# One matmul of 512 columns with a tile of high weights, or two of 256

## The reference, cut to what matters

```python
proj = u @ w_in[l]                       # 2048 x 9216, then attention and a convolution
... @ w_attn_o[l]; ... @ w_conv_o[l]     # 1024 x 2048 each
h = h + rms_norm(merged @ w_out[l], ...) # 2048 x 2048
gate, up = jnp.split(u @ w_gate_up[l], 2, axis=-1)   # 2048 x 11264
f = (jax.nn.silu(gate) * up) @ w_down[l]             # 5632 x 2048
h = x @ w_in                             # second block, even layer: 2048 x 6144
mixed @ w_out                            # 2048 x 2048
r, k, v, g = xr @ w_r, xk @ w_k, xv @ w_v, xg @ w_g  # odd layer: 2048 x 2048 each
(o + bonus) * silu(g) @ w_o                          # 2048 x 2048
```

## Time and profile before

| | |
|---|---|
| median of 3 runs | 2597.3 us (2593.73 to 2601.03) |
| profiled execution, first to last instruction (its span) | 2597.7 us |
| time of the profiled execution around its span | not recorded apart from the span; the runs and the span agree within 0.2% |
| TensorE matmul busy | 2502.5 us, 96% |
| TensorE weight load busy | 2160.8 us, 83% |
| VectorE busy | 1568.4 us, 60% |
| ScalarE busy | 1175.1 us, 45% |
| DMA | 427.69 MB, mean 165 GB/s |
| granted TensorE clock, mean | 0.988 of full speed |

### The profile page before, as it was taken

One profiled execution on the slowest core, in us unless ns is written; L12 is line 12 of the kernel. 1 busy time (PEld: TensorE's weight loads), 2 busy tenths in 40 slices (PEclk: granted clock), 3 DMA queues, 4 the chain that ended last, 5 costly groups with the idle time before them and its releaser, 6 DMA issues.

```text
span 2597.7 us, 38168 instructions
## 1 busy us (share of the span) xinstructions
PE 2502.5 (96%) x15470; PEld 2160.8 (83%) x15470; DVE 1568.4 (60%) x2116; ACT 1175.1 (45%) x1547; POOL 72.4 (3%) x94
## 2 busy tenths in 40 slices
PE   8999999999899999999999899989899999999896
PEld 7888888888788888888888688878787888888685
DVE  6888887774666655564444657655622674356555
ACT  5444554644444444444444355563546201255544
POOL 0000000000000000000000000000000201011000
PEclk9999999999999999999999999999999999999998
DMA  6564555555366566656555455545633457422362
GB/s 231 185 191 155 159 174 186 164 186 177 95 189 189 181 190 190 189 181 193 184 183 187 130 179 176 174 129 179 195 122 106 142 167 211 128 93 79 116 213 89
DMA packets 419455, 427.69 MB, mean 165 GB/s; under 512 B 25344, under 2 KB 414464, under 8 KB 418320
## 3 DMA queue, kind: packets, MB, share of 16 engines
q1 hardware_dynamic: 414880, 403.07, 49.0%
q0 software_dynamic: 4400, 22.19, 2.6%
HBM read 415.19 MB, written 9.96 MB: 164 GB/s over the span
## 4 chain that ended last, share of the span: by engine, by line
PE 84%; DVE 10%; ACT 4%; issue 1%; DMA 1%; SPq 0%; ACTq 0%; DVEq 0%
PE GP L1791 76%; PE SB L1791 7%; DVE wL L1011 3%; ACT wH L495 2%; DVE y L1011 1%; DVE acc L1017 1%; DVE x L1011 1%; DVE j L1011 1%; DVE f L1017 1%; DVE ga L1011 0%; PE SB L1795 0%; DMA raw<-w_o_dram 0%; DMA raw<-w_in_dram 0%; DVE xk L1017 0%; ACT sc L583 0%
## 5 line engine op out<-in xcount | busy, mean ns | idle before, releaser
L1011 DVE TENSOR_TENSOR wL<-raw,wH 128x1024 fp32r<-128x1024 f32 x664 | 805.1, 1226 | 581.6 <-ACT wH L495 580.0
L495 ACT CAST wH<-raw 128x1024 fp32r<-128x1024 f32 x664 | 685.8, 1048 | 564.9 <-PE GP L1791 323.9
L1791 PE MATMUL GP<-u2B,wH 128*128 128x512 f32 x1408 | 499.5, 399 | 0.0
L1791 PE MATMUL GP<-uB,wH 128*128 128x512 f32 x1152 | 409.6, 399 | 0.0
L1791 PE MATMUL GP<-u2B,wL 128*128 128x256 f32 x1408 | 398.3, 283 | 5.0 <-DVE u2B L1017 4.9
L1791 PE MATMUL GP<-uB,wL 128*128 128x256 f32 x1152 | 329.6, 286 | 4.3 <-DVE wL L1011 4.3
L1791 PEld LDWEIGHTS GP<-u2B,wH 128*128 128x128 f32 x1408 | 265.8, 189 | 65.4
L1791 PEld LDWEIGHTS GP<-u2B,wL 128*128 128x128 f32 x1408 | 267.3, 190 | 7.3 <-issue 4.3
L1791 PE MATMUL GP<-xB,wH 128*128 128x512 f32 x768 | 270.9, 395 | 0.0
L1791 PEld LDWEIGHTS GP<-uB,wH 128*128 128x128 f32 x1152 | 217.6, 189 | 52.4
L1791 PE MATMUL GP<-hB,wH 128*128 128x512 f32 x704 | 245.1, 392 | 0.0
(11 more groups left out here) (399 smaller groups left out, 3263.7 us busy)
## 6 DMA issues: line engine op xcount, KB each, us to landing
raw<-w_gate_up_dram SPq DMA_DIRECT2D x352, 256.0 KB, 3.7
raw<-w_in_dram SPq DMA_DIRECT2D x288, 256.0 KB, 3.4
raw<-ev_w_in_dram SPq DMA_DIRECT2D x192, 256.0 KB, 3.4
raw<-w_down_dram SPq DMA_DIRECT2D x176, 256.0 KB, 3.3
raw<-w_out_dram SPq DMA_DIRECT2D x64, 256.0 KB, 3.6
raw<-ev_w_out_dram SPq DMA_DIRECT2D x64, 256.0 KB, 3.4
dw<-w_k_dram SPq DMA_DIRECT2D x64, 256.0 KB, 3.3
dw<-w_r_dram SPq DMA_DIRECT2D x64, 256.0 KB, 3.2
```

What stands on the lines that cost most here:

```text
L495: e.copy(wH[SLOT[i]], raw[m % RAW].rearrange("p (k n) -> p k n", k=4)).then_inc(s["hi"], 1)
L1011: return e.tensor_tensor(o, a, b, op)
L1791: return e.matmul(o, l, r, start=start, stop=stop, skip_group_check=True)
```

## The change

In `stream`, the single 512-column matmul with the high weights becomes two of 256 columns with the same weights: one for the tokens' high half into `ps[:, c, 0, :]`, one for their low half into `ps[:, c, 1, :]`. The sums, the places and the order of accumulation into each place are the same. The end flag goes to both; the semaphore is raised by the second.

```diff
                             mm(ps[:, c, 0, :], l, xb[:, 0, kt, :], kt == 0, False)
-                            ins = mm(ps[:, c], h, xb[:, :, kt, :], False, kt == 4 * KUS[name] - 1)
+                            ended = kt == 4 * KUS[name] - 1
+                            mm(ps[:, c, 0, :], h, xb[:, 0, kt, :], False, ended)
+                            ins = mm(ps[:, c, 1, :], h, xb[:, 1, kt, :], False, ended)
                             if k == 3 and c == 1:
                                 ins.then_inc(s["unit"], 1)
```

## The result

The changed kernel takes 2639.4 us in the median (2638.9 to 2640.3) against 2597.3 (2593.7 to 2601.0): the ratio is 1.0157, 95% interval [1.0144, 1.0171], +42 us. The forecast was +15; the direction and the place were right, the size wasn't. The profiled execution has a span of 2636.8 us, 39.1 more than before, and took 2638.9 us.

A forecast was written before the change was run, and what follows sets the result against it. The prediction took TensorE's pace of starting stream matmuls as the bound. It weighted +6 us (117 ns matmuls) two thirds and +32 us (full-float32 cut) one third: 2597.7 + 15 gave 2612 us, forecast range 2603 to 2630, wider range 2572 to 2680.

The forecast's parts named there:

- instruction supply at nothing: Instruction queue q8: about 0.6 MB more traffic, priced at no time; +9 us if unexplained stalls grew with TensorE's instructions.
- Three of them make 351 ns: Streams: three 256-column matmuls at the low matmul's 117 ns, against 347 or 353 a step; together +6 us.
- the prediction's own sign: Check named beforehand: the stretch from 702 to 1170 us gets longer by no more than 3 us.
- The third of weight on full float32 cut in two: Second estimate from full-float32 matmuls, 216 ns whole and 222 in halves: +32 us over 5312 steps, weighted one third.
- every load costs: Rival, streams: each load's SBUF reading costs 11 or 14 ns, steps of 360 or 369, 2674 us; chance 0.10.
- Nothing changes: Rival, streams: the fp32r excess goes by column, not instruction, so 768 columns cost the same, 2597 us; chance 0.20.
- cost by the column alone: Streams: fp32r excess proportional to columns, 0.457 and 0.449 ns a column, because operands are read at full width each cycle.
- Faster: Rival, streams: the 512-column form stalls; all three pieces at 113 ns make 339 a step, 2540 us; chance 0.12.
- A shared reading limit: Rival, streams: operand and weight columns share an average 2.95 a ns, so 390 ns a step, 2811 us; chance 0.08.
- loads in a row: Rival, streams: full-length loads must follow one another, three of 190 ns making 570 a step, 3767 us; chance 0.03.
- not what it says: Rival, streams: the second load of the same high weights is left out, 2580 to 2597 us; chance 0.05.
- The cover that I priced at 1 us: Waits for weight tiles, 5% of the chain: units 0.7% longer give VectorE and ScalarE more cover, returning 1 us.

The follow-up runs named there:

- all64: All three matmuls of a step in the changed kernel use 64 of 128 weight columns, except in each slab's first row tile; ratio 0.9898 to the kernel before.
- both512: Kernel before, with the low weights too multiplied by both token halves, so two 512-column matmuls a step; 3119.9 us, ratio 1.2004.
- both512_64: Kernel before with two 512-column matmuls a step, both using 64 of 128 weight columns except in each slab's first row tile; ratio 1.2105.
- load64x2: Changed kernel with both high matmuls of a step using 64 of 128 weight columns, except in each slab's first row tile; ratio 1.0055 to the kernel before.
- load64_cols192: Changed kernel with the third matmul at 64 weight and 192 token columns, except in each slab's first row tile; ratio 0.9962 to the kernel before.
- cols192: Changed kernel with the third matmul taking 192 instead of 256 token columns, except in each slab's first row tile; ratio 0.9986 to the kernel before.

## Why the prediction was right or wrong

**Right:** the bound (the pace of TensorE in the streams), its weight (5.3 us for a nanosecond a step), the load of its own for each matmul and its cover by the matmul above, no change in clock, DMA or chain, and instruction supply at nothing: q8 went from 2.00 to 2.67 MB as counted, the waits for which the profile shows no cause fell from 54.0 to 47.9 us, and all64 ran the same instructions at 113.3 ns. All three starts at one distance, too.

**Wrong:** the term "Three of them make 351 ns". TensorE's pace does decide, and the added matmul does cost what a 256-column matmul costs; the price was too small: 120 ns, not 117, a step of 360. On 5312 steps that turns +6 us into +52. By the prediction's own sign the stretch should have grown by no more than 3 us; gate-up grew by 9.2. The third of weight on full float32 cut in two (+6 ns a cut) only lifted this towards the truth for another reason.

How 117 came to be wrong: it is the distance from a low matmul's start to the next start, in a pair that repeats in 346.7 ns, and the pair's excess over its columns isn't shared out fairly between its two distances. The prediction named the weakness, that each low matmul follows a long one with slack, but gave it no size. The pair was the number to use. 256 columns at 2.4 GHz are 106.7 ns, which both512 less the changed kernel measures (226.7 - 120). 768 columns are 320, the pair has 26.7 of excess for two matmuls, 13.3 for each; a third makes 360.0. The same 13.3 is left in 120 and in 226.7. This working was found after the result; both512 tested it (453 expected, 453.3 measured). It also needs the faster of the two paces: from gate-up's 353.3 it would give 370. I held the pieces of this in the rival "every load costs", but took the excess against full float32's 216 and 109 and not against the columns.

That rival, at 360 to 369, hit the pace in `w_down` (360) and missed in gate-up, where it added its cost to a base of 353; the changed kernel leaves that base behind, so the change cost 7 ns there and 12 to 13 elsewhere, and its 2674 us was further off than 2612. all64 shows that at 256 columns narrower loads take away half of the excess; both512_64, that at 512 they add to it. "Nothing changes" fell with the result, and its cost by the column alone with 453.3 for both512. "Faster": the 512-column form did hold a slower pace, as it said, but the pieces run at 120, not 113. "A shared reading limit" (390), "loads in a row" (570) and "not what it says" fell with the counts and paces above.

The rule of the Trainium skill in TensorE: Matmul & The Clock Gate, section Back-to-back issue gap, columns by 2.4 GHz plus 2.5 ns, is given there for a single matmul by itself, with no allowance for its load. By it a cut adds 2.5 ns (the prediction has 2.7), as an estimate +13 us. This case's traces have the slope (106.7 ns for 256 columns) and 13.3 instead of 2.5 as the fixed part in fp32r with full loads. The prediction saw agreement in full float32, but its 216 and 109 ns are matmuls of 256 and 128 columns, and the rule gives those times for 512 and 256. A smaller slip of reading is without effect: the 32 matmuls of `BKW` start in pairs, so there are fifteen distances and not sixteen, the first of 213 ns and the others near 112.

The cover that I priced at 1 us gave back 10. The unit grew by 2.8%, not 0.7%, which by the same proportion is 4 us; the rest shows that a share of the chain is no measure of what a longer unit covers. So the two errors worked against each other: without the second the change would have cost 52 us. The prediction also said that waits on VectorE or ScalarE moving by more than 10 us would make its argument wrong; the idle stretches moved by just that, and the pace alone doesn't give the total.

Open: why the fixed part is 13.3 with full loads and 6.7 with narrow ones at 256 columns, yet larger with narrow ones at 512; why one narrow load in three (350) is faster than two (353.4); and what the slower pace comes from.

## What to carry to other kernels

Price a repeating pattern by its period, not by the distance from one of its members to the next: subtract the columns' time from the whole period, divide the rest by the number of matmuls, and multiply by the new number. In fp32r with full loads that rest was 13.3 ns a matmul here, so halving a 512-column matmul cost 13.3 ns, 6% of its 226.7, although every load ran under a matmul; keep the moving operand as long as the bank allows. Don't carry the 13.3 to other load widths or formats: with narrower loads it was anything from 6.7 (all64) to 16.7 (both512_64), and my forecasts for load64x2, load64_cols192 and both512_64 missed. And look whether a long stream runs at one pace everywhere: if the same instructions take 347 ns here and 353 there, the base is not settled, and a change may seem cheaper or dearer for leaving it.

## What the runs showed of the hardware that was not expected

- Steady fp32r streams repeat after whole multiples of 6.67 ns, at paces that last for hundreds of steps (1356 of them, 479 us, in the kernel before). Two foreign matmuls (0.43 us) ended the slower pace in two cases of three, and single distances longer by 0.1 us started it; its cost was 6.7 ns in 346.7, 1.9%.
- A narrower weight load isn't always cheaper: two of 64 columns instead of two of 128 raised two 512-column matmuls from 453.3 to 460 ns.
- A full load took 108 ns before the next load and 115 before its matmul even under a 192-column matmul, so that matmul saved 11 ns instead of 27 (cols192).
- bf16 operands taken as every second element of the same words, with full 128-column loads, ran at 113.3 ns where fp32r ran at 120; their loads' records are 96 ns instead of 192.
